# Forgetting attention: a new order of TensorE's work inside a pair of heads

## The reference, cut to what matters

```
q, k, v, g = h @ w_in                      # 1024 x 1024 each
q, k       = rms_norm(q), rms_norm(k)      # per head
logits     = q k^T / sqrt(64) + c[t] - c[s]     for s <= t   # c = cumsum(log f)
out        = softmax(logits) v
result     = (out * silu(g)) @ w_out
```

## Time and profile before

| | |
|---|---|
| runs of the kernel before | 1547.44, 1548.29, 1540.58 us |
| the profiled execution | 1539.76 us, of which the span from first to last instruction is 1538.0 us |
| TensorE matmul busy | 1412.2 us, 92% of the span |
| VectorE, ScalarE busy | 949.0 us (62%), 711.9 us (46%) |
| mean granted TensorE clock | 0.973 of full |
| the forgetting attention's 8 pairs | 1134.3 us to 1417.0 us of the span |
| one pair (of pairs 0 to 6) | 36.3 us |

### The profile page before, as it was taken

One profiled execution on the slowest core, in us unless ns is written; L12 is line 12 of the kernel. 1 busy time (PEld: TensorE's weight loads), 2 busy tenths in 40 slices (PEclk: granted clock), 3 DMA queues, 4 the chain that ended last, 5 costly groups with the idle time before them and its releaser, 6 DMA issues.

```text
span 1538.0 us, 18015 instructions
## 1 busy us (share of the span) xinstructions
PE 1412.2 (92%) x6912; PEld 1182.8 (77%) x6912; DVE 949.0 (62%) x1324; ACT 711.9 (46%) x940; POOL 81.7 (5%) x81
## 2 busy tenths in 40 slices
PE   4798889999989999999979999999789999996996
PEld 3687777888868888888868898787667777775875
DVE  6798786444354444444478776536776677777365
ACT  4677767332232223232346444335365666556251
POOL 3000000000300000000020000021100000000202
PEclk9999999999989999999989999999899999997998
DMA  5111011322212232322221121222121111111211
GB/s 191 56 55 56 1 55 55 110 90 101 105 60 84 108 108 82 109 82 101 91 82 55 55 107 58 96 85 108 55 82 55 55 55 55 55 55 69 82 55 55
DMA packets 19237, 118.16 MB, mean 77 GB/s; under 512 B 2400, under 2 KB 3680, under 8 KB 5616
## 3 DMA queue, kind: packets, MB, share of 16 engines
q1 hardware_dynamic: 18896, 116.38, 21.3%
q0 software_dynamic: 288, 1.05, 0.2%
HBM read 115.32 MB, written 2.10 MB: 76 GB/s over the span
## 4 chain that ended last, share of the span: by engine, by line
PE 64%; DVE 17%; ACT 12%; issue 6%; DVEq 0%; DMA 0%; ACTq 0%
PE ps L500 20%; PE ps L502 19%; PE ps L501 19%; DVE wlo L1598 2%; ACT whi L1046 1%; PE ps L683 1%; ACT fq L1046 1%; PE ps L953 1%; ACT fka L1046 1%; DVE acc L376 1%; DVE att L1843 1%; DVE nmax L2166 1%; PE ps L564 1%; ACT pthi L1046 1%; ACT att L1165 1%
## 5 line engine op out<-in xcount | busy, mean ns | idle before, releaser
L500 PE MATMUL ps<-uhi,whi 128*128 128x512 f32 x1168 | 466.7, 400 | 12.4 <-DVE ulo L1647 6.0
L502 PE MATMUL ps<-uhi,wlo 128*128 128x512 f32 x1168 | 457.8, 392 | 0.0
L501 PE MATMUL ps<-ulo,whi 128*128 128x512 f32 x1168 | 457.4, 392 | 0.0
L1598 DVE TENSOR_TENSOR wlo<-wraw,whi 128x2048 fp32r<-128x2048 f32 x105 | 240.2, 2290 | 109.2 <-ACT whi L1046 107.6
L1046 ACT ACTIVATE whi<-wraw 128x2048 fp32r<-128x2048 f32 x105 | 200.4, 1908 | 182.2 <-PE ps L502 182.0
L500 PEld LDWEIGHTS ps<-uhi,whi 128*128 128x128 f32 x1168 | 221.4, 190 | 65.2 <-issue 15.8
L502 PEld LDWEIGHTS ps<-uhi,wlo 128*128 128x128 f32 x1168 | 220.8, 189 | 47.5
L501 PEld LDWEIGHTS ps<-ulo,whi 128*128 128x128 f32 x1168 | 221.7, 190 | 45.3 <-issue 1.9
L500 PE MATMUL ps<-hdhi,whi 128*128 128x512 f32 x256 | 99.6, 389 | 0.0
L501 PE MATMUL ps<-hdlo,whi 128*128 128x512 f32 x256 | 99.6, 389 | 0.0
L502 PE MATMUL ps<-hdhi,wlo 128*128 128x512 f32 x256 | 99.6, 389 | 0.0
(11 more groups left out here) (391 smaller groups left out, 2354.8 us busy)
## 6 DMA issues: line engine op xcount, KB each, us to landing
wraw<-wstream SPq DMA_DIRECT2D x105, 1024.0 KB, 4.7
h<-xT SPq DMA_DIRECT2D x4, 512.0 KB, 5.5
outT<-pp SPq DMA_DIRECT2D x8, 256.0 KB, 2.2
s5b<-s5p_d SPq DMA_DIRECT2D x1, 1024.0 KB, 12.1
pe_in<-pT POOLq DMA_DIRECT2D x2, 512.0 KB, 3.6
cst_in<-cst_d SPq DMA_DIRECT2D x5, 64.0 KB, 10.2
reset<-cst_d SPq DMA_DIRECT2D x1, 256.0 KB, 11.4
ones<-cst_d SPq DMA_DIRECT2D x1, 64.0 KB, 2.6
```

The source lines that it names most:

```text
L500: nc.tensor.matmul(out, lh, rh, start=start, stop=False, skip_group_check=True)
L501: nc.tensor.matmul(out, lh, rl_, start=False, stop=False, skip_group_check=True)
L502: mm = nc.tensor.matmul(out, ll, rh, start=False, stop=stop, skip_group_check=True)
L1598: V.tensor_tensor(wlo[:, slot, :], wraw[:, slot, :], whi[:, slot, :], ALU.subtract).then_inc(lo_done, 1)
```

## The change

Two edits on TensorE and one on VectorE, in the loop and in the last pair alike (where the projections are absent):

- TensorE issues `scores(1)` ahead of `transpose_probs(0)`. As both heads use `zf`, a wait is put before it until ScalarE has finished all three groups of `exps(0)`.
- The v block of the next pair is cut in two: its first two of eight steps (6 matmuls) are issued between `weigh_values(0)` and `transpose_probs(1)`, and the other six steps (18 matmuls) stay where the block stood. The wait for both copies out of banks 0 and 1 becomes one for the copy out of bank 0, and stands ahead of the first part.
- VectorE does `row_max(1)` before `probs_lo(0)`.

```diff
                 scores(0)
                 if not last:
                     gemm(i * 2 + (U_FOX + 2), U_FOX % 2, one(0), 256, uhi, ulo)
+                pe.wait_ge(exp_done, i * 6 + 3)
+                scores(1)
                 transpose_probs(0)
-                scores(1)
                 if not last:
                     pe.wait_ge(g_copy, i + 1)
                     gemm(i * 2 + (U_FOX + 2), U_FOX % 2, one(1), 256, uhi, ulo)
                 weigh_values(0)
+                if not last:
+                    pe.wait_ge(qk_copy, i * 2 + 3)
+                    gemm(i * 2 + (U_FOX + 3), (U_FOX + 1) % 2, one(0), 256, uhi, ulo, part=range(2))
                 transpose_probs(1)
                 if not last:
                     fox_qk_sums(i + 1)
-                    pe.wait_ge(qk_copy, i * 2 + 4)
-                    gemm(i * 2 + (U_FOX + 3), (U_FOX + 1) % 2, one(0), 256, uhi, ulo)
+                    gemm(i * 2 + (U_FOX + 3), (U_FOX + 1) % 2, one(0), 256, uhi, ulo, part=range(2, DC))
                 weigh_values(1)
@@ VectorE
                 normalise(0)
+                row_max(1)
                 probs_lo(0)
-                row_max(1)
                 normalise(1)
```

## The result

The changed kernel is slower. Over 20 runs each, its median is 1549.67 us (1545.95 to 1559.83) and that of the kernel before 1547.07 us (1540.58 to 1549.07). The ratio of the means is 1.0035, 95% interval 1.0018 to 1.0051, so about 5.4 us; the medians are 2.6 us apart. Mean and median differ because the runs of the changed kernel form two groups: ten take 1545.95 to 1548.31 us, with a mean clock of 0.965 to 0.967 of full, and ten take 1551.03 to 1559.83 us, with 0.958 to 0.964. The forecast was 0.15% faster, 1545.1 us: wrong in sign.

The account below looks back on a forecast made before the run. A cycle of waits over ScalarE, VectorE and TensorE was taken to bound each pair, at 36.29 us. Seven pairs each 0.33 us shorter gave 2.3 us off the 1547.44 us median: 1545.1 us, range 1536 to 1551.

Parts of the forecast that it names:

- The ring: Closed chain of waits over a pair through ScalarE, VectorE and TensorE: 36.29 us, forecast to become 35.96 us.
- part one: From the start of head 1's transposes to the end of the next exps(0), on ScalarE and VectorE: 24.16 us, unchanged.
- T: Start of the transposes of head 1 in a pair: 1154.83 in pair 0, 1191.12 in pair 1 before.
- Part two, steps 1 to 7: TensorE's order from the end of exps(0) to the next head 1 transposes: 12.13 us, forecast 0.33 us shorter.
- Step 1: Added wait before scores(1): ScalarE's release reaches TensorE 0.13 us after exps(0) ends.
- The v part costs inside the ring: Six v matmuls before head 1's transposes take 1.37 us and remove a wait of 1.01 us: -0.36 us.
- The new waits: TensorE idles 0.4 to 0.5 us before scores(0), for fkb, and about 1.8 us before scores(1), for exps(0).
- the sum: Gain over pairs 0 to 6, 7 x 0.33 = 2.3 us, taken off 1547.44 us to give 1545.1 us.
- the clock falls in each pair: Rival: TensorE runs at 1.2 GHz after the pause before scores(1); +13.4 us, 1560.9 us; chance 0.06.
- a sign of being wrong: Observation listed as showing the forecast wrong: a clock under 1.00 in pairs 1 to 6.
- The last pair: Pair without projection blocks: change costed at 0, with -2 to +2 us if its clock changes fall otherwise.
- won as a whole: Rival: each pair wins all that leaves TensorE's list, 1.70 us, 11.9 us over seven pairs, 1535.5 us; chance 0.11.

Follow-up runs that it names:

- both single-edit kernels: Two kernels, each with one TensorE edit against the kernel before: head order alone, ratio 0.9976; v block cut in two alone, ratio 1.0068.
- vpart_only: Only the v block cut in two, heads in the old order, against the kernel before: seven pairs sum to 261.95 us, ratio 1.0068.
- after_again: The changed kernel profiled and run again, nothing edited: pairs of 36.07 to 36.08 or 37.66 to 37.70 us, ratio 1.0031 to the kernel before.
- before_again: The kernel before profiled again, nothing edited: 1548.63 us, seven pairs sum to 253.99 us.
- the k steps: Changed kernel with two or three k block steps moved before the exponentials' wait: ratios 0.9948, 0.9919; two steps with the v block whole: 0.9945.
- rowmax_back: The changed kernel with VectorE's edit undone, row_max(1) again after probs_lo(0): ratio 1.0047 to the kernel before.
- order_only: Only the head order and early row maxima, v block whole, against the kernel before: seven pairs sum to 250.01 us, ratio 0.9976.
- filler: The changed kernel with six useless k block matmuls per pair added ahead of the wait for the exponentials: pairs sum to 252.51 us, ratio 1.0003.

## Why the prediction was wrong

**The ring, part one** (24.16 us from T on ScalarE and VectorE): right. After, from the transposes at 1202.76 to the next row maxima at 1224.01 it is 21.25 us; before, from 1154.83 to 1176.13, 21.30.

**Part two, steps 1 to 7** (0.33 us earlier): right, a little too large. Where the clock is full a pair takes 36.08, 0.2 less than before and not 0.33. Step 1 was sized too small: the scores started 1189.50 - (1188.97 + 0.21) = 0.32 us after `exps(0)` ended, and I had taken 0.13 from the store of `og`. The split of it is also right: -0.57 for the order (36.28 to 35.71) against a forecast of 0.69, less that late release, and +0.37 for the v part against 0.36.

**The v part costs inside the ring**: right, shown by both single-edit kernels.

**The new waits**: right, place and size.

**Where it failed: the sum took every pair at full clock, on the argument that set the rival "the clock falls in each pair" at 0.06.** The clock was under 1.00 in pairs 1 to 6, a sign of being wrong that the prediction itself names, and that put 6 x 1.6 us where the sum has nothing. I read that a gap of 2.90 us without a matmul had kept 1.00 and took a pause of 1.8 us to be safe. One row of a gap that had no consequence doesn't make gaps of that length harmless: pauses of 1.75 to 1.81 us with the same code around them had a fall behind them in all six pairs with such a pause in one execution and in 4 of 6 in another. The premise itself doesn't hold either: behind that very gap the clock fell in `vpart_only`. The rule from the Trainium skill's "TensorE: Matmul & The Clock Gate" that I weighed and set aside is right in kind, pauses cost the clock. The Trainium skill's table there, under "Why this matters for your kernels", warns only of gaps that are longer; here 1.78 us was too much, and the measurement decides.

**The rival's price was too high.** I had 2.25 us of full-speed work lost, from a window of 4.5 us in the last pair. The stretch is 3.4 us and costs 37.69 - 36.08 = 1.6 us. With six falls less seven gains this is 6 x 1.6 - 7 x 0.2 = +8.2, as the sums say (262.17 - 253.94). Priced like this and counted in the two profiled executions, the rival gives +5 to +8 us, not +13.4.

**The last pair** was set at 0, with -2 to +2 us for its clock. The profiled executions have 22.44 us from its first row maxima to the store of head 1 after, and 23.45 before: within that. In `after_again` and `before_again` it is 24.37 and 24.20, so no gain from the early `exps(1)` can be told from the scatter.

**Between the other rivals**: "won as a whole" (34.6 us a pair) was rightly held off; the ring closes over VectorE and ScalarE, and only the k steps, which take work out of the ring's part two, brought such pairs.

## What to carry to other kernels

Moving work forward to fill one pause makes another: work out where TensorE then idles, and how long in one piece. The total doesn't tell it: TensorE idles 2.1 us in a pair of before and 2.1 us in a full-clock pair of the changed kernel, but in pieces of up to 1.2 us there and of 1.8 us here. And one pause that went well in one trace is no proof: look for the same pause in other executions first. A part that is put in front of a wait costs its own length in the ring if it is longer than the wait (1.37 for 1.01). If a wait can't go, give it the work that stands right behind it in the ring, as the k steps here: it shortens the ring, and it keeps the clock.

## What the runs showed of the hardware

- A fall of the clock cost 1.6 us of time for a stretch of 3.4 us at 1.2 GHz where it lay in the ring, 1.2 to 1.5 us in `vpart_only`, and nothing where TensorE had slack. In the pairs of the loop falls came behind pauses of 1.75 to 1.94 us only, 18 times out of 24 (6 of 6 in the changed kernel; 4 of 6 in `after_again`, in `rowmax_back` and in `vpart_only`). Pauses of 1.0 to 1.5 us (both executions of before, `order_only`, and pair 0 of the three traces with the changed order and the v part) and of 0.4 us (filler) had none.
- Length alone doesn't decide: behind the pause of 2.9 us ahead of the attention the clock fell in 1 of 11 traces.
- The falls aren't independent draws. In the changed kernel's first profile the fall begins 1.38 us after the end of the pause in pair 1 (1189.50 to 1190.88) and 0.69 us in pair 6 (1377.93 to 1378.62), some 0.14 us less with each pair; in `after_again` the last of the row begins 0.8 us after it, and the next pair has none. In `vpart_only` pairs 2, 3, 5 and 6 fell, 0.2 to 0.8 us after the pause. What decides between two equal pauses was not tried.
- More matmuls in less time: six useless ones per pair made a pair 1.6 us shorter than with a fall, and no longer than one without (36.07 and 36.08 us).
